# Row sums from the transposed input, and a bias mirrored before it is spread out, in a hybrid attention block

## The reference

```python
h = rms_norm(x, norm_gain)                    # 1 / sqrt(mean(x*x) + 1e-6) for each token
proj = h @ w_in                               # 2048 -> 9296, split in qa ka va ga qb kb vb gb qi ki wi
s_a = qa @ ka.T * 128**-0.5 + rel_bias[head, clip(q - k, -128, 128) + 128]   # 8 heads, chunk-causal, softmax
score = sum_h(wi * relu(qi @ ki.T)); sel = top_k(score, 64)                  # an indexer picks 64 keys
s_b = qb @ kb.T * 128**-0.5 - slope[head] * |q - k|                          # 8 heads over these keys, softmax
y = concat(p_a @ va * silu(ga), p_b @ vb * silu(gb))
out = rms_norm(x + y @ w_out, final_gain)
```

## Time and profile before

| | |
|---|---|
| time, median of 3 runs | 555.32 us (555.07 to 557.23) |
| the profiled execution | 555.07 us |
| its span, first to last instruction | 552.9 us |
| PE busy | 538.4 us, 97% |
| DVE busy | 324.2 us, 59% |
| ACT busy | 254.8 us, 46% |
| POOL busy | 29.5 us, 5% |
| DMA | 103.65 MB, 187 GB/s |

### The profile page before, as it was taken

How to read it: one execution, slowest core, us unless ns; L and a number is a source line. 1 busy time by engine, 2 the same in 40 slices (tenths; PEclk the granted TensorE clock), 3 DMA queues, 4 the chain that set the end, 5 groups by cost and what they waited for, 6 DMA issues and landing times.

```text
span 552.9 us, 7916 instructions
## 1 busy us (share of the span) xinstructions
PE 538.4 (97%) x2536; PEld 447.2 (81%) x2536; DVE 324.2 (59%) x461; ACT 254.8 (46%) x353; POOL 29.5 (5%) x40
## 2 busy tenths in 40 slices
PE   7998999999999999999999999999999999999994
PEld 4877888888888888888888888888888888888883
DVE  5845456656565566666565555466565648556464
ACT  6774444444444444434544434443544445554332
POOL 1000220202000000000010101010100000000000
PEclk9999999999999999999999999999999999999998
DMA  8966555456655556555544454454554566565613
GB/s 282 420 258 206 175 163 191 149 183 209 208 162 183 189 196 194 198 195 163 191 152 152 161 176 156 156 167 144 188 168 165 167 203 238 191 193 180 207 67 152
DMA packets 28863, 103.65 MB, mean 187 GB/s; under 512 B 3360, under 2 KB 3760, under 8 KB 28464
## 3 DMA queue, kind: packets, MB, share of 16 engines
q1 hardware_dynamic: 27936, 96.82, 52.4%
q0 software_dynamic: 768, 6.31, 3.2%
q10 hardware_dynamic: 144, 0.33, 0.2%
HBM read 101.34 MB, written 2.11 MB: 187 GB/s over the span
## 4 chain that ended last, share of the span: by engine, by line
PE 91%; DMA 4%; DVE 1%; ACT 1%; issue 1%; SPq 1%; DVEq 0%; ACTq 0%
PE acc L342 27%; PE acc L344 27%; PE acc L343 27%; DMA v<-x 2%; PE aux L370 2%; PE aux L490 1%; PE aux L466 1%; DMA qk<-xT 1%; DMA w_raw<-w_blocks 1%; PE aux L405 1%; PE aux L435 1%; DVE w_lo L803 1%; PE aux L494 1%; PE aux L469 1%; PE aux L479 1%
## 5 line engine op out<-in xcount | busy, mean ns | idle before, releaser
L803 DVE TENSOR_TENSOR w_lo<-w_raw,w_hi 128x1024 fp32r<-128x1024 f32 x174 | 215.6, 1240 | 193.7 <-ACT w_hi L583 193.5
L583 ACT ACTIVATE w_hi<-w_raw 128x1024 fp32r<-128x1024 f32 x174 | 184.4, 1060 | 253.9 <-PE acc L344 248.7
L342 PE MATMUL acc<-w_hi,a_hi 128*128 128x512 f32 x704 | 278.4, 395 | 2.1 <-DVE w_lo L803 1.1
L344 PE MATMUL acc<-w_hi,a_lo 128*128 128x512 f32 x704 | 274.4, 390 | 0.0
L343 PE MATMUL acc<-w_lo,a_hi 128*128 128x512 f32 x704 | 274.3, 390 | 0.0
L342 PEld LDWEIGHTS acc<-w_hi,a_hi 128*128 128x128 f32 x704 | 132.3, 188 | 30.7 <-issue 3.5
L344 PEld LDWEIGHTS acc<-w_hi,a_lo 128*128 128x128 f32 x704 | 132.2, 188 | 28.1
L343 PEld LDWEIGHTS acc<-w_lo,a_hi 128*128 128x128 f32 x704 | 132.4, 188 | 25.8
L315 POOL TENSOR_TENSOR q_now<-qk,qscale 128x512 f32<-128x512 f32 x8 | 12.0, 1501 | 271.0 <-PE aux L469 233.3
L693 ACT ACTIVATE p<-p,neg_max 128x256 f32<-128x256 f32 (+1 forms) x32 | 14.1, 442 | 0.7 <-DVE neg_max L982 0.7
L370 PE MATMUL aux<-ident,stage 128*128 128x128 f32 x80 | 10.4, 272 | 2.6 <-DVE stage L811 2.6
(11 more groups left out here) (121 smaller groups left out, 263.3 us busy)
## 6 DMA issues: line engine op xcount, KB each, us to landing
w_raw<-w_blocks SPq DMA_DIRECT2D x142, 512.0 KB, 3.3
w_raw<-wo_blocks SPq DMA_DIRECT2D x32, 512.0 KB, 3.7
v<-x POOLq DMA_DIRECT2D x2, 2048.0 KB, 9.9
qk<-xT SPq DMA_DIRECT2D x7, 256.0 KB, 6.7
w_raw<-w_blocks SPq DMA_DIRECT2D x4, 256.0 KB, 4.2
o<-ext_dram POOLq DMA_DIRECT2D x1, 1024.0 KB, 6.7
fgain<-final_gain POOLq DMA_DIRECT2D x1, 1024.0 KB, 6.7
out<-o SPq DMA_DIRECT2D x2, 512.0 KB, 3.0
```

Source lines behind the costliest of these rows:

```text
L342: nc.tensor.matmul(dst, a_hi[:, k, t], hi, start=start, stop=False)
L344: return nc.tensor.matmul(dst, a_lo[:, k, t], hi, start=False, stop=stop)
L583: nc.scalar.activation(flat(w_hi[:, s, :, :]), w_raw[:, s, :], ACT.Copy).then_inc(hi_done, 1)
L803: nc.vector.tensor_tensor(flat(w_lo[:, s, :, :]), w_raw[:, s, :], flat(w_hi[:, s, :, :]).bitcast(f32), ALU.subtract).then_inc(lo_done, 1)
```

## The change

Three things change. The sum of squares is taken from the pieces of xT: POOL squares each piece (two slices, 128x512) and adds it to a sum in `o`, and after unit(1,0) PE sums over the partitions with four matmuls against a column of ones; the load of x at L284 and ACT's two squares go, and the splits of units 8 to 13 move around the root accordingly. The bias row is mirrored by DVE when it lands, in a second small copy; POOL then, after the last split of the indexer's queries, writes all shifted windows from SBUF to DRAM (1 MB), waits, and loads them in their final place; the two reversed copies go. The parts of the last rows are cut otherwise.

```diff
-        VECTOR_PARTS = ((0, slice(0, D // 2)), (0, slice(D // 2, D)), (1, slice(0, CB)), (1, slice(CB, 2 * CB)),
-                        (1, slice(2 * CB, 1408)))
-        SCALAR_PART = slice(1408, D)
+        sq_sum, sq_x = o_flat[:, 0:UK * T], o_flat[:, UK * T:2 * UK * T]
+        VECTOR_PARTS = ((0, slice(0, D // 2)), (0, slice(D // 2, D)), (1, slice(0, CB)), (1, slice(2 * CB, D)))
+        SCALAR_PART = slice(CB, 2 * CB)
@@ POOL
-            pool.dma_start(bias_ext[:, 0:2 * MAX_REL + 1], rel_bias).then_inc(row_landed, 16)
+            pool.dma_start(bias_row[:, :], rel_bias).then_inc(row_landed, 16)
...
-            pool.wait_ge(xT_landed[UNITS - 1], 16)
-            pool.dma_start(x_nat, x).then_inc(x_landed, 16)
-            pool.wait_ge(ext_ready, 1)
-            pool.dma_start(ext_dram, bias_ext[:, :]).then_inc(ext_stored, 16)
+            pool.wait_ge(xT0_landed, 16)
+            for u in range(UNITS):
+                pool.wait_ge(xT_landed[u], 16)
+                x_u = flat(xT_land[:, UK * u:UK * u + UK, :])
+                if u == 0:
+                    nc.gpsimd.tensor_tensor(sq_sum, x_u, x_u, ALU.mult).then_inc(sq_step, 1)
+                    continue
+                pool.wait_ge(sq_step, 2 * u - 1)
+                nc.gpsimd.tensor_tensor(sq_x, x_u, x_u, ALU.mult).then_inc(sq_step, 1)
+                pool.wait_ge(sq_step, 2 * u)
+                nc.gpsimd.tensor_tensor(sq_sum, sq_sum, sq_x, ALU.add).then_inc(sq_step, 1)
...
             split_q(0)
-            pool.wait_ge(ext_stored, 16)
-            windows = bass.AP(tensor=ext_dram.tensor, offset=ext_dram.offset + 1,
-                              ap=[[1, P], [3 * P, HEADS], [1, T]])
-            pool.dma_start(bias_back, windows).then_inc(bias_landed, 16)
             for i in range(1, 4):
                 pool.wait_ge(iscored, 2 * i)
                 split_q(i)
+            pool.wait_ge(ext_ready, 2)
+            ext = bias_ext[:, :]
+            windows = bass.AP(tensor=ext.tensor, offset=ext.offset + P - 1, ap=[list(ext.ap[0]), [-1, P], [1, T]])
+            pool.dma_start(bias_dram.rearrange("p h c -> h p c"), windows).then_inc(ext_stored, 16)
+            pool.wait_ge(ext_stored, 16)
+            pool.dma_start(bias[:, :, :], bias_dram).then_inc(bias_landed, 16)
             pool.dma_start(fgain[:, :], final_gain.partition_broadcast(P)).then_inc(fgain_landed, 16)
@@ PE
             unit(1, 0)
+            pe.wait_ge(sq_step, 2 * UNITS - 1)
+            for m in range(TM):
+                for k in range(UK):
+                    last = nc.tensor.matmul(aux[1][:, m:m + 1], sq_sum[:, k * T + m * P:k * T + m * P + P],
+                                            ones[:, :], start=(k == 0), stop=(k == UK - 1))
+            last.then_inc(ssq_done, 1)
@@ ACT
-            split_hi(0, 8)
-            split_hi(0, 9)
-            act.wait_ge(x_landed, 16)
-            for m in range(TM):
-                if m > 0:
-                    act.wait_ge(ssq_done, m)
-                nc.scalar.activation(o_flat[:, 0:D], x_nat[:, m, :], ACT.Square,
-                                     accum_out=ssq[:, m:m + 1]).then_inc(ssq_done, 1)
-                split_hi(0, 10 + m)
+            for c in (8, 9, 10):
+                split_hi(0, c)
...
             nc.scalar.activation(rstd[:, :], ssq[:, :], ACT.Sqrt).then_inc(std_done, 1)
-            split_hi(0, 12)
+            for c in (11, 12):
+                split_hi(0, c)
@@ DVE
-            last_bias = bias_ext[:, 2 * MAX_REL:2 * MAX_REL + 1]
-            nc.vector.tensor_copy(bias_ext[:, 2 * MAX_REL + 1:3 * P],
-                                  last_bias.broadcast_to((HEADS, P - 1))).then_inc(ext_ready, 1)
+            last_bias = bias_row[:, 2 * MAX_REL:2 * MAX_REL + 1]
+            nc.vector.tensor_copy(bias_ext[:, 0:P - 1], last_bias.broadcast_to((HEADS, P - 1))).then_inc(ext_ready, 1)
+            nc.vector.tensor_copy(bias_ext[:, P - 1:3 * P], bias_row[:, ::-1]).then_inc(ext_ready, 1)
...
-            for c in range(8, 12):
+            for c in (8, 9, 10):
                 split_lo(0, c)
-            dve.wait_ge(ssq_done, 2)
-            nc.vector.tensor_scalar(ssq[:, :], ssq[:, :], 1.0 / D, EPS, ALU.mult, ALU.add).then_inc(var_done, 1)
+            dve.wait_ge(ssq_done, 1)
+            nc.vector.tensor_scalar(ssq[:, :], aux[1][:, 0:TM], 1.0 / D, EPS, ALU.mult, ALU.add).then_inc(var_done, 1)
...
-            for c in (12, 13):
+            for c in (11, 12, 13):
                 split_lo(0, c)
...
             dve.wait_ge(bias_landed, 16)
-            for h in (0, HEADS // 2):
-                nc.vector.tensor_copy(bias[:, h:h + HEADS // 2, :],
-                                      bias_back[:, h:h + HEADS // 2, ::-1]).then_inc(bias_turned, 1)
-            dve.wait_ge(bias_turned, 2)
             nc.vector.memset(bias[0:HALF, :, T - CHUNK:T], MASKED).then_inc(bias_masked, 1)
```

More of the change, by code:

```diff
@@ L97, in hybrid_block @@
         bias_ext = sb("bias_ext", [HEADS, 3 * P])
+        bias_row = sb("bias_row", [HEADS, 2 * MAX_REL + 1])
         neg_slope = sb("neg_slope", [P, HEADS])
@@ L150, in hybrid_block @@
         nlo_done = sem("nlo_done")
-        x_landed = sem("x_landed")
+        sq_step = sem("sq_step")
         ssq_done = sem("ssq_done")
@@ L172, in hybrid_block @@
         pen_step = sem("pen_step")
-        bias_turned = sem("bias_turned")
         bias_masked = sem("bias_masked")
@@ L195, in hybrid_block @@
         vector_scaled = sem("vector_scaled")
-        ext_dram = nc.dram_tensor("ext_dram", (HEADS, 3 * P), f32, kind="Internal").ap()
+        bias_dram = nc.dram_tensor("bias_dram", (P, HEADS, T), f32, kind="Internal").ap()
         AUX01_INDEX, AUX01_PAIRS, AUX01_Y = 2, 10, 18
@@ L208, in hybrid_block @@
         o_flat = o[:, :, :, :].rearrange("p b m c -> p (b m c)")
-        bias_back = o_flat[:, D:2 * D].rearrange("p (h k) -> p h k", h=HEADS)
         qnow_flat = flat(q_now[:, :, :])
```

## The result

The changed kernel takes 571.61 us (571.16 to 571.73, 4 runs), the kernel before 555.72 us (555.07 to 557.23, 4 runs): ratio 1.0286, 95% interval 1.0269 to 1.0304. It is slower, as forecast (565.7), but by 15.9 us and not 10.4, and outside the range of 557.5 to 569. The profiled execution has a span of 570.6 us against 552.9. That is 17.7 us and not 15.9: the profile of before is its shortest execution (555.07), and the spans of the changed kernel's executions lie between 569.2 and 570.7.

A forecast was written before the change was run, and what follows sets the result against it. PE was taken to bound the kernel, busy 97% of the span. Head +13.05 + 0.9 − 3.6 = +10.35, bias and tail 0; 552.9 + 10.35 + 2.17 = 565.4, plus 0.25 to the median: 565.7 us, range 557.5 to 569.

The forecast's parts named there:

- sign: Whole kernel: the change makes it slower, chance 0.85, against 0.08 faster and 0.07 the same.
- the bound for the bias: Bias store and load of 1 MB each: delay to PE by competing with weight loads, 0 to 0.5 us, taken as 0.
- the ring: Buffered weight units loaded ahead of ACT; with 2 MB of x loading beside them, PE had lost under 0.4 us.
- Even 10 times that hides: POOL's queue at the bias: a 1 MB load lands after 6.7 us, and PE needs q_now only after 87 us.
- the case given 0.04: Head: PE loses clock by working half the time to 32 us; time over 569 us, chance 0.04.
- The turns: Head: POOL and DVE operations with two SBUF operands exclude each other and alternate one for one; +13.05 us, chance 0.62.
- DVE wins when both wait: Head, rival: DVE's splits keep near their times and POOL gets the holes; 559 to 561.2 us, chance 0.19.
- the work hides: Head, rival: POOL's squares are cheap beside the splits, PE finds the sums ready; 552.6 us, chance 0.13.
- the prediction's own short hold: Head: POOL keeps DVE out 0.88 us per operation if a square reads as little as L294; 1.13 was taken.
- The small matmuls: Head, PE: four float32 matmuls with one moving column for the new sums cost 0 to 0.9 us, taken as +0.9.
- The gap before the transposes: Head, PE before L370: the time lost waiting for block_out goes, −3.60 us.
- The tail: End of kernel: ACT's and DVE's last parts are cut otherwise; change 0, within 0.3 us.

The follow-up runs named there:

- head_only: Only the sums of squares of the change (POOL squares, four PE matmuls, moved splits) put into the kernel before, bias path and tail as before; 561.77 us, ratio 1.0087.

## Why the prediction was wrong

Its sign and its mechanism in the head held; one step failed, and one was mis-sized. The two errors point in opposite directions: 10.5 us too little for the bias, 3.1 too much for the head.

- **The failed step**: "the bound for the bias is 0 to 0.5 us; ... I take 0". The argument was that 2 MB of `x` beside the weights had cost PE under 0.4 us, so 1 MB would cost no more. It priced a transfer by its bytes. This one comes from 8 partitions: it took 25.2 us to land, the weight units beside it 19.9, and that is past what the ring covers. It cost 10.5 us in the profile and 9.2 as a kernel of its own. "Even 10 times that hides" was true for POOL's queue and was never asked of the ring. The range left the case out; the text named the place (132 to 165 us) where a gap would prove it wrong, and there it was. The measured time lies beyond 569, as in the case given 0.04, but for another reason than that case names.
- **The turns** held. From 9.6 to 29.5 us there are 13 operations of POOL and 13 of DVE between them, the `a_lo` in pairs of 2.68 us; "DVE wins when both wait" is out, and so is "the work hides". That an `a_lo` behaves as a `w_lo` does was an assumption; it is shown.
- **Their size** was too large: +7.24 and not +10.35. The split of unit 4 ended at 28.4 instead of 31.9. Of these 3.5 us the squares are 2.0: they take 1.04 us and not 1.29, so that reading the same operand twice costs what L294 does, and by the prediction's own short hold that is 8 x 0.25 of the 16.95 us. POOL's second operation waited for its piece of `xT` until 8.52, and DVE passed two operations meanwhile. So only 14 POOL operations came before this split and not 15 (1.13 us less by the prediction's hold), but neither engine had a turn from 7.7 to 8.5 (0.8 more). POOL began 0.3 earlier. The remaining 0.9 us are spread over the turns. Then unit(0,4) started at 28.52 instead of 32.05, and from there PE took 14.0 us for five units, not 13.6: 9.85 us in place of 13.05.
- The small matmuls: 0.80 us, forecast 0.9. The gap before the transposes went: 3.41 us, forecast 3.60. 9.85 + 0.80 − 3.41 = 7.24.
- The clock, given 0.04 as a case of its own, fell twice: 0.68 in 20 to 24 us, which cost nothing because PE waited 1.61 us for DVE behind it anyway, and for 5 us behind the long idle, 2.6 us of the bias's price.
- The tail, "0, within 0.3": −0.29 in the profile.

With the head at its measured 7.2 and nothing else the forecast would have been 562.6, inside the range, and `head_only` measured 561.77; the bias alone put the result outside.

## What to carry to other kernels

Before handing elementwise work to an idle POOL, look whether DVE is busy there with operations on two SBUF operands: they take turns, one for one, so POOL's idle share is no free time, and a short DVE operation pays most (two `a_lo` in 2.68 us instead of 0.88). Price a transfer by how many partitions it comes from as well as by its bytes, and hold its landing against the cover of each ring that shares the DMA engines. A wait of PE on which its next unit doesn't depend is cheapest to remove by order: one moved line gave about as much (ratio 0.9939) as the sums of squares could give if they cost DVE nothing (0.9931).

## What the runs showed of the hardware

- A DRAM store of 1 MB in runs of 1 KB landed after 25.0, 13.5 and 8.1 us from 8, 16 and 32 partitions, and 6.5 from 128, all from POOL's queue; from 8 partitions and ACT's queue it took 25.2.
- While the store from 8 partitions ran, weight units of 512 KB landed after 19.9 us instead of 3.3, and all DMA together moved 111 GB/s, with the engines 0.71 busy.
- After 7.6 us of idle PE ran matmuls of 512 columns 0.43 us apart for 5 us, at a granted clock of 0.54 to 0.61 in the windows, and then 0.23.
- With work of two SBUF operands waiting on both, POOL and DVE took turns one for one: 13 operations of each between 9.6 and 29.5 us.
- POOL's product of an operand with itself takes 1.04 us for 512 columns, the sum of two, with DVE taking turns, 1.32 at least; a fill of 1024 columns 0.96.
